# Turning the normalised rows in two halves, and three small pieces of work around it, in a one-core transformer block

## The reference

```
x = x + attention(rms_norm(x))                    # first block
x = x + swiglu(rms_norm(x))
for l in (0, 1):                                  # second block
    h = rmsnorm(x) * g * (1 + scale_l) + shift_l  # "norm 2" for l = 0
    l = 0: y = mlstm(h): proj = h @ w_in (with 16 gate columns); matrix memory with gates;
               head norm; sigmoid(o) * .. * silu(z); @ w_out
    l = 1: kv = modulate(rmsnorm(x, kv_g), ..) @ kv_w          # "norm 3", on the same x
           y = band_attention(h, kv) @ w_out
    x = x + gate_l * rmsnorm(y, g_post_l)         # "post"
```

## Time and profile before

| | |
|---|---|
| median of 3 runs | 2470.12 us |
| profiled execution, its own time | 2470.29 us |
| its span in the trace | 2468.5 us |
| granted TensorE clock, mean | 0.994 |
| PE busy | 98% |
| DVE, ACT, POOL busy | 71%, 47%, 2% |
| HBM | 233 GB/s |

### The profile page before, as it was taken

How to read it: one execution, slowest core, us unless ns; L and a number is a source line. 1 busy time by engine, 2 the same in 40 slices (tenths; PEclk the granted TensorE clock), 3 DMA queues, 4 the chain that set the end, 5 groups by cost and what they waited for, 6 DMA issues and landing times.

```text
span 2468.5 us, 30282 instructions
## 1 busy us (share of the span) xinstructions
PE 2424.4 (98%) x11068; PEld 1979.9 (80%) x11068; DVE 1741.2 (71%) x2446; ACT 1163.8 (47%) x1563; POOL 49.5 (2%) x69
## 2 busy tenths in 40 slices
PE   9999999999999999799999999999999999999998
PEld 7777888888888888578888888888888778888886
DVE  7785777777777776567677667677676676666665
ACT  6665444444443444454444434444444554455553
POOL 1100000000000000000000000000000000000000
PEclk9999999999999999999999999999999999999999
DMA  8435888888888887367777787777777557776664
GB/s 286 137 120 157 268 289 289 305 296 295 287 291 294 295 289 231 106 205 235 244 230 238 239 264 237 245 232 238 235 231 241 149 178 244 248 237 211 230 194 130
DMA packets 161826, 578.11 MB, mean 234 GB/s; under 512 B 18288, under 2 KB 20592, under 8 KB 161680
## 3 DMA queue, kind: packets, MB, share of 16 engines
q1 hardware_dynamic: 160432, 572.64, 70.8%
q0 software_dynamic: 1104, 3.28, 0.4%
q10 hardware_dynamic: 144, 0.26, 0.0%
HBM read 574.01 MB, written 2.10 MB: 233 GB/s over the span
## 4 chain that ended last, share of the span: by engine, by line
PE 81%; issue 11%; DVE 4%; ACT 2%; DMA 1%; POOL 0%; SPq 0%; DVEq 0%; POOLq 0%; ACTq 0%
PE PS L1055 25%; PE PS L1057 25%; PE PS L1056 25%; PE PS L698 1%; DVE WL L2004 1%; ACT WH L1409 1%; PE PS L790 0%; PE PS L763 0%; DVE X L1974 0%; DMA cols<-in_cols 0%; PE PS L886 0%; PE PS L906 0%; DVE AR L1516 0%; PE PS L907 0%; PE PS L903 0%
## 5 line engine op out<-in xcount | busy, mean ns | idle before, releaser
L2004 DVE TENSOR_TENSOR WL<-W,WH 128x1024 fp32r<-128x1024 f32 x816 | 993.2, 1224 | 550.7 <-ACT WH L1409 547.7
L1409 ACT ACTIVATE WH<-W 128x1024 fp32r<-128x1024 f32 x816 | 859.6, 1060 | 930.0 <-PE PS L1057 923.5
L1055 PE MATMUL PS<-WH,XTH 128*128 128x512 f32 x2144 | 858.8, 401 | 11.4 <-DVE WL L2004 7.9
L1057 PE MATMUL PS<-WH,XTL 128*128 128x512 f32 x2144 | 837.6, 391 | 0.0
L1056 PE MATMUL PS<-WL,XTH 128*128 128x512 f32 x2144 | 836.6, 390 | 0.0
L1055 PEld LDWEIGHTS PS<-WH,XTH 128*128 128x128 f32 x2144 | 403.7, 188 | 102.2 <-issue 22.7
L1057 PEld LDWEIGHTS PS<-WH,XTL 128*128 128x128 f32 x2144 | 403.3, 188 | 86.3
L1056 PEld LDWEIGHTS PS<-WL,XTH 128*128 128x128 f32 x2144 | 404.1, 188 | 83.0 <-issue 3.8
L1055 PE MATMUL PS<-WH,YTH 128*128 128x512 f32 x1120 | 443.5, 396 | 8.9 <-DVE WL L2004 5.4
L1057 PE MATMUL PS<-WH,YTL 128*128 128x512 f32 x1120 | 438.1, 391 | 0.0
L1056 PE MATMUL PS<-WL,YTH 128*128 128x512 f32 x1120 | 437.9, 391 | 0.0
(11 more groups left out here) (273 smaller groups left out, 1166.3 us busy)
## 6 DMA issues: line engine op xcount, KB each, us to landing
W<-in_vec SPq DMA_DIRECT2D x192, 512.0 KB, 4.5
W<-in_avoz SPq DMA_DIRECT2D x192, 512.0 KB, 4.4
W<-in_wg SPq DMA_DIRECT2D x88, 512.0 KB, 4.7
W<-in_wu SPq DMA_DIRECT2D x88, 512.0 KB, 4.7
W<-in_wd SPq DMA_DIRECT2D x88, 512.0 KB, 4.7
W<-in_gate SPq DMA_DIRECT2D x64, 512.0 KB, 4.6
W<-in_aqk SPq DMA_DIRECT2D x64, 512.0 KB, 4.5
W<-in_aout SPq DMA_DIRECT2D x64, 512.0 KB, 4.4
```

What stands on the lines that cost most here:

```text
L1055: e.matmul(p, x, WH[:, g % NH, j], start=first, stop=False)
L1057: i = e.matmul(p, y, WH[:, g % NH, j], start=False, stop=last)
L1409: e.activation(WH[:, n % NH], W[:, i % NW], ACT.Copy).then_inc(s_hi, 1)
L2004: e.tensor_tensor(l, src, h.bitcast(F32), ALU.subtract).then_inc(s_lo, 1)
```

## The change

- Mean and epsilon of a norm are one DVE instruction (`tensor_tensor_reduce` of four sums with ones).
- The gate weights' DMA and the masks stand before norm 2 on POOL, and the split of the gate weights (`gate_w`) at the start of the third group of the feed-forward block; the task `gates` starts in the middle of `first_rows`, four ticks earlier in the order, and its later steps have other distances.
- Columns 0 to 1023 are turned as before by quarters (pieces 0, 1 for t = 0, then 4, 5 for t = 1). Columns 1024 to 2047 are turned for all 256 rows at once, in pieces 12 to 15 of 256 columns, behind the rows t = 1 of norm 2 and 3 and within the next slots; shifting such a piece takes two instructions of 128x256.
- A piece can be spread over two banks, the first shifted by ACT and the second by DVE (`BY_ACT` gives the number of parts of ACT; `banks_of`, `pieces`).
- In norm 2 a bank is released when the upper part is written and no longer when the shift is done.
- The last gate product is made by VectorE in front of `post` (`gated`) and not by POOL; at the very end it reads PSUM directly, as ACT's squares do there, and the copy to YA is left out.
- In norm 3 the square sum of the last 512 columns of the first half is made by DVE, and the order of posts, squares and weight preparation is another; 12 warming products instead of 14.

```diff
-    def bank(n, i):
-        raw = [("raw", i)] if n == 3 else []
-        return ([("turned", n, i)] + (raw if i >= 4 else []) + [("shifted", n, i), ("upper_T", n, i)]
-                + (raw if i < 4 else []) + [("lower_T", n, i)])
     def norm_2(second_rows, second_out):
...
         yield ("scaled", 2, 1)
+        yield from second_rows(mid={2: [("turned", 2, 0)]}, after={2: [("turned", 2, 1)]})
+        yield ("shifted", 2, 0)
+        yield ("upper_T", 2, 0)
         yield ("lower", g + 1)
-        yield from second_rows({2: [("turned", 2, 0), ("turned", 2, 1)]})
...
     def norm_3(second_rows, second_out):
...
         yield from second_rows()
+        yield ("mean_x", 3, 0)
+        yield ("upper", g + 2)
         yield second_out()
...
+        yield ("scaled", 3, 0)
+        yield ("warm", 12)
+        yield ("turned", 3, 0)
+        yield ("lower", g + 1)
         yield ("mean_y", 0, 1)
...
+        yield ("gated", 0, 1, None)
         yield ("shifted", 3, 0)
         yield ("upper_T", 3, 0)
+        yield ("scaled", 3, 1)
+        yield ("turned", 3, 1)
+        yield ("lower_T", 3, 0)
+        yield ("upper", g + 3)
+        yield ("lower", g + 2)
         yield ("post", 0, 1, 0)
...
+    def first_rows(name, n, need):
...
+        begin = [("start", "gates", g)] if n == 2 else []
+        yield from rows(name, range(4), par, 8, need, 0, mid={3: [("turned", n, 4)]}, after={
+            0: [("scaled", n, 4), ("scaled", n, 5)],
+            3: [("turned", n, 5), ("shifted", n, 4), ("upper_T", n, 4), ("scaled", n, 2), ("lower_T", n, 4)]
+            + raw(0, 1) + [("shifted", n, 5), ("upper_T", n, 5), ("scaled", n, 6), ("lower_T", n, 5)] + begin})
+        yield from rows(name, range(4), par, 8, need, 1, after={
+            0: fill[1] + raw(4, 5) + [("scaled", n, 3), ("scaled", n, 7), ("turned", n, 12)],
+            1: fill[2] + later(n, 12), 2: fill[3] + [("turned", n, 13)], 3: later(n, 13) + [("turned", n, 14)]})
+    def later(n, i):
+        return [("shifted", n, i), ("upper_T", n, i), ("lower_T", n, i)] + ([("raw", i)] if n == 3 else [])
+    def rest(name, n, need):
+        return chunk(name, need, k0=4, after={4: later(n, 14) + [("turned", n, 15)], 5: later(n, 15)})
...
+        if gi == 2:
+            yield ("gate_w", free)
...
+BY_ACT = {(2, 0): 2, (2, 1): 4, (2, 4): 2, (2, 5): 4, (2, 12): 2, (2, 13): 2, (2, 14): 2, (2, 15): 2,
+          (3, 0): 4, (3, 1): 4, (3, 4): 2, (3, 5): 4, (3, 12): 2, (3, 13): 0, (3, 14): 2, (3, 15): 0}
...
+            def gated(p, t, par):
+                y = YA[:, t, 1536:2048]
+                w.wait_ge(s_row, 4 * p + 4)
+                step(e.tensor_tensor(y, Gb[par][t][:, :] if p else y, GG[:, 1536:2048], ALU.mult))
```

More of the change, by code:

```diff
@@ L227, in rows @@
                 yield half(g, name, k, j, par, k == 0, k == nk - 1, need(2 * k + j, t), (t,), end)
+                if j == 0:
+                    yield from mid.get(n, ())
             yield ("tick",)
@@ L333, in norm_3 @@
+        yield ("lower_T", 3, 1)
+        yield ("lower", g + 3)
         yield ("post", 0, 1, 2)
         yield ("post", 0, 1, 3)
-        yield ("lower_T", 3, 1)
-        yield ("lower", g + 3)
         yield ("mean_x", 3, 1)
-        yield ("raw", 0)
-        yield ("raw", 1)
-        for i in (4, 5, 2, 6, 3, 7):
-            yield ("scaled", 3, i)
-        yield from first_rows("Y", 3, banks(YT_KV), 2)
-    def first_rows(name, n, need, turn_at):
-        late = [bank(n, i) for i in range(8)]
+        yield from first_rows("Y", 3, banks(YT_KV))
@@ L347, in first_rows @@
+    def first_rows(name, n, need):
         g = at["g"]
         par = at["chunk"] % 2
-        yield from rows(name, range(4), par, 8, need, 0, {turn_at: late[4], 3: late[5]})
+        raw = lambda *o: [("raw", i) for i in o] if n == 3 else []
         fill = [[("upper", g + x), ("lower", g + x)] for x in range(4)]
-        yield from rows(name, range(4), par, 8, need, 1, {0: late[2], 1: late[6] + fill[1], 2: late[3] + fill[2],
-                                                          3: late[7] + fill[3]})
+        begin = [("start", "gates", g)] if n == 2 else []
[6 more added lines that the diff above has]
+            1: fill[2] + later(n, 12), 2: fill[3] + [("turned", n, 13)], 3: later(n, 13) + [("turned", n, 14)]})
@@ L402, in score @@
             if h == 0 and c == 0:
-                yield from chunk("X", banks(16), k0=4)
+                yield from rest("X", 2, banks(16))
             else:
@@ L415, in score @@
         if j == 0:
-            yield from chunk("Y", banks(YT_KV), k0=4)
+            yield from rest("Y", 3, banks(YT_KV))
         else:
@@ L823, in gates @@
                     if k < 7:
-                        yield
+                        yield from ticks(1 if k < 4 else 2)
                 i.then_inc(full, 1)
@@ L1128, in shifted @@
+                for src, dst, scale, shift in pieces(n, i, b, xs_):
+                    o = e.activation(dst, src, ACT.Identity, scale=scale, bias=shift)
                 o.then_inc(s_ats, 1)
             def raw(i):
-                t, c = i // 4, i % 4
-                b = full(("norm", 3, i))
                 w.wait_ge(s_sum, 6)
-                e.activation(RAW[c][:, :, 128 * t:128 * t + 128], b[:, :].rearrange("p (a k) -> p a k", a=4),
-                             ACT.Copy).then_inc(s_raw, 1)
+                if i < 8:
+                    t, c = i // 4, i % 4
+                    dst = RAW[c][:, :, 128 * t:128 * t + 128]
+                else:
+                    dst = RAW[(i - 8) // 2][:, 2 * (i % 2):2 * (i % 2) + 2]
@@ L1381, in scalar_program, with out @@
             added = [0]
-            def out(what, c, par, _, ts):
+            def out(what, c, par, g, ts):
                 for t in ts:
-                    if what in ("aout1", "bout"):
+                    if what == "bout" and c == 3:
+                        w.wait_ge(s_rows_t if ts == (0,) else s_unit, g)
+                        square(Gb[par][t][:, :], ssy[:, 4 * t + c:4 * t + c + 1])
+                    elif what in ("aout1", "bout"):
                         n = ("aout0", "aout1", "bout").index(what)
@@ L1440, in scalar_program @@
                     out(*a)
-                elif what == "post" and a[0] == 0:
+                elif what == "gate_w":
+                    gate_w(a[0])
+                elif what == "post" and a[0] == 0 and a[1:] != [0, 3]:
                     w.wait_ge(s_post, 4 * a[1] + a[2] + 1)
@@ L1953, in out @@
                         e.tensor_tensor(y, y, p, ALU.add).then_inc(s_ya, 1)
+                    elif what == "bout" and c == 3:
+                        continue
                     elif what in ("aout0", "bout"):
@@ L2085, in vector_program @@
                     post(*a)
+                elif what == "gated":
+                    gated(*a)
+                elif what == "gate_w":
+                    gate_w(a[0])
         def gpsimd_program(e):
```

204 lines of the change are left out of this document (105 added, 99 removed).

## The result

The changed kernel takes 2450.14 us (median of 4 runs, 2449.58 to 2450.44), the kernel before in the same job 2470.07 (2469.72 to 2471.49): ratio 0.9918, 95% interval 0.9901 to 0.9935, so 19.9 us faster. In a later job the same two took 2449.62 and 2471.08. The forecast was 2448, with 2443 to 2457 around it. The profiled execution took 2450.33 us, its span 2448.6.

A forecast was written before the change was run, and what follows sets the result against it. PE was taken as the bound, so gains could come only where it waits: norm 2, gate chain, norm 3, tail. -16.5 - 3 + 0 - 2.4 = -21.9 us from 2470.1 gave 2448; 8-in-10 range 2443 to 2457.

The forecast's parts named there:

- Norm 2 and the gate chain: Norm 2 to the convolutions behind the gates: -16.5 us from shorter PE stands, -3 from an earlier scan.
- The hand schedule: The changed order of each engine laid out by hand on measured instruction durations, giving start times and stands in the norms.
- The masks at nothing: POOL's masks, moved from norm 2 to about 442 us, were booked as an edit worth 0.
- Norm 3: Norm 3: gains and new stands in front of slots 664 to 667 cancel; value 0, ends -4 and +5 us.
- a sign of being wrong: Listed as showing the forecast wrong: PE waiting for ACT's raw copies in norm 3; no size given.
- The tail: Behind the last product: -2.4 us, 1.4 from the dropped copy and 1.0 from POOL's absence.
- Rival 1: Norm 2's 7 us gate stand moves to late pieces: norm 2 gives 10, norm 3 loses 2; 2457 us, 13%.
- Rival 2: Norm 3: squares before the shift, bank wait and slow stretches coincide, +5; gate chain no gain; 2456 us, 9%.
- Rival 3: Norms 2 and 3: transposes waiting for bank releases hold PE's queue, 12 pieces make +32; 2480 us, 3%.
- Rival 4: Gate step in norm 2 waits for something other than its weights, so the stand returns; 2458 us, 3%.

The follow-up runs named there:

- e12: Changed kernel with norm 2's six `scaled` back where they stood before the change, between slot 342's and slot 343's weight rests: 2452.50 us.
- e1: Changed kernel with the whole gate task and its weights begun where they were before, behind slot 343's rows; masks stay early: 2456.26 us.
- e3: Changed kernel with the masks' memset and select put back behind POOL's powers of norm 2: 2450.26 us.
- e2: Kernel before, with only the gate weights made at slot 268 and their DMA and the masks issued ahead of POOL's powers: 2461.24 us.
- e9: Changed kernel, unaltered, run once more: 2449.62 us.
- e4: Changed kernel with the last product's half quarter again copied to SBUF by DVE, then squared and multiplied there; POOL stays silent: 2451.82 us.
- e5: Changed kernel with ACT's square in norm 3 moved behind its shift and upper part of piece 1: 2447.34 us.
- e11: Changed kernel with e5's move, slot 663's weight piece early, and raw copies of pieces 0 and 1 behind the squares: 2444.09 us.
- e6: Changed kernel with norm 2's six `scaled` put in front of slot 342's weight rest too, further forward than before the change: 2455.36 us.

## Why the prediction was right, point by point

**Norm 2 and the gate chain: -19.5 forecast, -18.60 measured.** The hand schedule, moved by the 1.20 us: second half's rows of slot 340 predicted 1003.95, measured 1003.93; slot 342 998.95 and 998.66; the first half of slot 344 through at 1014.7, measured 1015.08. Cut the piece at the first product of slot 345: before it came 37.2 us behind the second half's last product, with two gate steps done, and now 22.8, with five. At 0.70 us a step norm 2 gives 14.4 + 2.1 = 16.5, where 16.5 was forecast. That leaves 2.1 for the chain, where 3 was forecast: it stood 0.26 + 1.02 us (forecast 0.7) for 2.24, and has one slow stretch less. Three terms were found by taking them out: order of `scaled` (e12, 3.9), early gate weights with their place (e1, 6.7), masks (e3, 1.0). These 11.7 are not the 18.6: each was taken out of the finished order, and what the pieces for all rows and the two banks gave in norm 2 was not tried alone.

**The masks at nothing** was the step that failed, without harm. The prediction saw the row (`scaled` 0.69 beside the memset) and even used 0.43 in the new order, so the gain is inside its -16.5; but it booked the masks' move as free of effect instead of naming it as a term of 1.0 us (e3) or 1.1 (e2: 1.7 of one stand less 0.6 of a new one). In their new place behind 442 us they cost nothing on the path: PE has no wait at all between 430 and 480 us.

**Norm 3: 0 forecast, +0.26 measured**, and here two errors met. The stands stood where the schedule put them: slot 662 at 1972.85 forecast, 1954.91 + 17.63 = 1972.54 measured; 663 at 1977.4 and 1977.02; slots 664 to 667 stood 0.7, 0.8, 0 and 1.3 for 1.3, 1.4, 0.4 and 1.8; the wait for the bank came as foreseen, though the same text names that wait as a sign of being wrong. So the last four stands were 2.1 us too long in the forecast, and the slow stretches, three of them, were not in it. e9 has the same code in 50.18, with two stretches. But the code of before varies likewise: e2 leaves norm 3 as it was and takes 49.97 with two. Compared at the same count the term is +0.2 (two) or +0.3 (three). "0" is right within that, by two errors that cancel, which is luck.

**The tail: -2.4 forecast, -2.51 measured**, and split as forecast. Without the copy ACT's square starts 0.43 us behind the last product instead of 1.90, which gives 1.47 (forecast 1.4). The posts without POOL beside them gain 3.73 - 2.74 = 0.99 (forecast 1.0), and mean and power the last 0.05. e4 gets only 0.72 of the 1.47 back because before the copy also waited: it started 0.76 us after the product was usable, when DVE was through with the other half's posts, and these too are shorter now.

**The rivals.** Rival 1, the stand moves, shows in no run: the 7.04 us go whole in the old order (e2), and in the new one no stand lies between 1004 and 1037 us. Rival 2's three conditions came true in norm 3 (squares in front of the shift, the bank, three slow stretches) and cost 0.2 to 0.3 net, because the stands of before went in the same breath, and before had three stretches too; e5 and e11 give the prices of the first two, 1.55 and 0.8. Rival 3, PE's queue standing for bank releases: one stand of 0.99 us, not twelve. Rival 4: the row is gone.

**The +1.2 us ahead of norm 2** was in nobody's sum: a slow stretch behind a stand at 160 us, in code that the change does not touch. With it -19.9, without it -21.1, against -21.9.

## What to carry to other kernels

- Cut the run at instructions that both kernels have at the same place of the work, and compare the pieces. Here 1322 of 2450 us repeat within some hundredths, so a change of 1 us is seen in its own piece where the times of one kernel (2448.46 to 2450.60) can't show it.
- Price a new stand of PE with its slow stretch, some 1.4 us where PE is busy through it: e1's theory had left out two, 2.8 of its 6.7 us. But take it away again where PE stands or another engine is behind: in norm 3 three stretches cost 1.1 us more than one, not 2.8.
- Before a stand is called new, look for it at the same slot of the kernel before: e2's 1.89 us looks like the 7.04 us moved, and had been there as 1.90.
- Where a wait names the engine that makes weights, look in its queue for what stands in front and itself waits. A square that waits for a post, or a mean that waits for another engine, costs the wait as well as its own time (e5, e6).
